# Redistributing table tiles over steps, and the order of VectorE and ScalarE work in the second pass, in a PEER layer

## What is computed

```python
q = (xb @ w_q).reshape(TOKEN_BLOCK, PEER_HEADS, 2, PEER_HALF)      # 8 heads
s1, s2 = scores of q[:, :, 0] and q[:, :, 1] with 128 keys each
v1, i1 = top_k(s1, 16); v2, i2 = top_k(s2, 16)
top_s, pos = top_k(v1[..., :, None] + v2[..., None, :], 16)
idx = i1 * 128 + i2 at pos                                          # one of 16384 experts
gate = softmax(top_s)
act = gelu(einsum('td,thkd->thk', xb, expert_u[idx]))
out = einsum('thk,thkd->td', gate * act, expert_v[idx])
x = layer_norm(alpha * x + out)
```

## Time and profile before

| | us |
|---|---|
| median of 3 runs (3006.0 to 3010.39) | 3006.27 |
| the profiled execution | 3014.1 |
| its span on the core | 3012.3 |

### The profile page before, as it was taken

How to read it: one execution, slowest core, us unless ns; L and a number is a source line. 1 busy time by engine, 2 the same in 40 slices (tenths; PEclk the granted TensorE clock), 3 DMA queues, 4 the chain that set the end, 5 groups by cost and what they waited for, 6 DMA issues and landing times. The chain is left out here.

```text
span 3012.3 us, 53462 instructions
## 1 busy us (share of the span) xinstructions
PE 2616.7 (87%) x20618; PEld 1518.2 (50%) x20618; DVE 2327.7 (77%) x4875; ACT 1223.7 (41%) x3048; POOL 971.8 (32%) x888
## 2 busy tenths in 40 slices
PE   9899978787887767768888869999998997999997
PEld 7677433232332333323333326666676775766774
DVE  7965577999879899976767867767788884877776
ACT  3254143233345555533333423333244332544454
POOL 0000144444445555544343522223232222211221
PEclk9999999889997777779998989999999999999998
DMA  4113699999999999999999989999999999999995
GB/s 165 63 56 140 240 403 419 413 404 417 412 419 405 420 411 420 419 420 421 421 418 406 419 336 383 397 394 401 400 416 375 397 412 411 386 392 369 410 393 210
DMA packets 175382, 1100.76 MB, mean 365 GB/s; under 512 B 17829, under 2 KB 34341, under 8 KB 52778
## 3 DMA queue, kind: packets, MB, share of 16 engines
q0 software_dynamic: 110592, 805.36, 65.3%
q1 hardware_dynamic: 64554, 292.16, 24.5%
HBM read 1061.79 MB, written 35.65 MB: 364 GB/s over the span
## 5 line engine op out<-in xcount | busy, mean ns | idle before, releaser
L975 POOL DMA_INDIRECT arena_high<-uv_dram,idx_now x768 | 929.3, 1210 | 1665.9 <-PE ps L1258 1525.2
L2430 DVE SCALAR_TENSOR_TENSOR arena_high<-arena_low,arena_high 128x1024 f32<-128x1024 f32 x768 | 922.4, 1223 | 267.4 <-DMA arena_high<-uv_dram,idx_now 261.5
L1258 PE MATMUL ps<-arena_high 32*32 32x512 f32 x12288 | 493.5, 671 | 282.5 <-ACT arena_high L1815 278.1
L1496 PE MATMUL ps<-arena_low 128*128 128x256 f32 x2048 | 463.7, 382 | 0.0
L1496 PEld LDWEIGHTS ps<-arena_low 128*128 128x128 f32 x2048 | 384.0, 190 | 109.4 <-issue 46.0
L1806 ACT ACTIVATE gcol<-hcol 128x2 f32<-128x2 f32 x384 | 77.6, 202 | 824.4 <-DVE arena_high L2430 820.0
L1258 PEld LDWEIGHTS ps<-arena_high 32*32 32x32 f32 x12288 | 94.8, 107 | 481.6 <-ACT arena_high L1815 384.6
L1219 PE MATMUL ps<-arena_low 128*128 128x512 f32 (+1 forms) x512 | 242.0, 616 | 14.3 <-DMA arena_low<-slabs_dram 14.3
L332 PE MATMUL ps<-wv_hi_bytes,w_hi_bytes 128*128 128x512 f32 x512 | 207.6, 406 | 19.4 <-DVE v_lo_bytes L2554 13.1
L1815 ACT ACTIVATE arena_high<-arena_high,wcol 128x32 f32<-128x32 f32 x768 | 204.9, 314 | 12.5
L334 PE MATMUL ps<-wv_hi_bytes,w_lo_bytes 128*128 128x512 f32 x512 | 202.3, 395 | 0.0
(11 more groups left out here) (264 smaller groups left out, 4002.4 us busy)
## 6 DMA issues: line engine op xcount, KB each, us to landing
arena_low<-ut_dram SPq DMA_DIRECT2D x64, 1024.0 KB
arena_high<-vt_dram SPq DMA_DIRECT2D x32, 1024.0 KB, 12.7
arena_low<-vt_dram SPq DMA_DIRECT2D x32, 1024.0 KB
arena_low<-spread_dram SPq DMA_DIRECT2D x32, 512.0 KB
acts_dram<-arena_low SPq DMA_DIRECT2D x14, 1024.0 KB
arena_low<-acts_dram SPq DMA_DIRECT2D x28, 512.0 KB
arena_low<-slabs_dram SPq DMA_DIRECT2D x11, 1152.0 KB
arena_high<-uv_dram,idx_now POOLq DMA_INDIRECT x768
```

The lines of the kernel that those rows point to most:

```text
L975: pool.indirect_dma_start(out=ring[:, s % RING, :], out_offset=None, in_=uv_d, in_offset=bass.IndirectOffsetOnAxis(ap=idx_now[:, s:s + 1], ...
L1258: last = nc.tensor.matmul(ps[out:out + QUAD, y_bank(t // PH) + turn, :], diag[rows, s % DIAGS, :], ring[rows, s % RING, cs], start=fresh, ...
L1496: last = nc.tensor.matmul(ps[:, 5 + n % 4 // 2, o:o + 2 * P], u_slot[n % USLOTS][:, k, :], x1T[:, BLK - DENSE:BLK, k, :], start=(k == 0), ...
L2430: last = nc.vector.scalar_tensor_tensor(out=ring[:, s % RING, 0:D], in0=x1[c][:, j, :], scalar=1.0, in1=ring[:, s % RING, 0:D], op0=ALU.mu ...
```

## The change

The steps are shared out anew. `TAIL` goes from 3 to 7 and `V_STEPS` from 31 to 29, which leaves `U_STEPS` = 92. The first table's tiles are no longer spread evenly: `u_share` gives a step 133, 193 or 95 parts (some 1.35, 1.96 or 0.96 tiles): 133 up to s = 55, 193 for s = 56 to 64 and 83 to 91, and 95 for s = 65 to 82. In the latter stand now all 64 groups, 18 steps instead of 24, with `hot` in 4 places, VectorE one step ahead of the other engines, and the group's work before the table tile on TensorE and ScalarE. One slab load and the first four `load_g` come earlier in SyncE's program. From s = 91 to s = 120 VectorE and ScalarE do `dense` at the beginning of a step, before the row products.

```diff
-TAIL = 3
-V_STEPS = 31
+TAIL = 7
+V_STEPS = 29
...
-G_STEP0 = PICK0 + DENSE * PH * PICK_PARTS - U0
-G_STEPS = 24
+G_STEP0 = PICK0 + DENSE * PH * PICK_PARTS - U0 + 1
+G_STEPS = 18
+HOTS = 4
 KEPT = 2
+G_BACK = G_STEP0 + G_STEPS + 4
...
+def u_share(s):
+
+    G = U0 + s
+    if G < PICK0 + 7 * STEPS:
+        return 133
+    return 95 if G_STEP0 <= s < G_STEP0 + G_STEPS else 193
+
 def u_first(s):
-    return NT * s // U_STEPS
+    return NT * sum(u_share(i) for i in range(s)) // sum(u_share(i) for i in range(U_STEPS))
...
+def second_pass(G):
+    return U_STEPS - 1 <= G - U0 < U_STEPS + V_STEPS
...
             for n in range(NT):
+                if n == USLOTS - 2:
+                    for half in range(2):
+                        load_slab_late(LATE_SLAB + 2, half)
                 if n % 2 == 0:
                     load_u(n // 2)
...
+                if n == u_first(G_BACK) + USLOTS:
+                    for c in range(2):
+                        for part in range(2):
+                            load_g(c, part)
...
-            for c in range(2):
-                for part in range(2):
-                    load_g(c, part)
...
             def dense(s):
 
-                if s == G_STEP0:
+                if s == G_STEP0 - 1:
                     for j in range(DENSE):
                         turn_picks(j)
-                if 0 <= s < U_STEPS:
-                    for n in range(u_first(s), u_first(s + 1)):
-                        u_tile(n)
                 o = s - G_STEP0
                 if 0 <= o < G_STEPS:
                     for i in range(g_first(o), g_first(o + 1)):
                         g_group(i)
+                if 0 <= s < U_STEPS:
+                    for n in range(u_first(s), u_first(s + 1)):
+                        u_tile(n)
...
+                    if second_pass(t * STEPS + g):
+                        dense(t * STEPS + g)
                     expert_weights(t, g, steps)
...
-                    dense(t * STEPS + g)
+                    if not second_pass(t * STEPS + g):
+                        dense(t * STEPS + g)
...
-                if i >= 2:
-                    wait_again(dve, g_psum, i - 1)
+                if i >= HOTS:
+                    wait_again(dve, g_psum, i - HOTS + 1)
...
-                o = s - G_STEP0
+                o = s - G_STEP0 + 1
...
+                    if second_pass(t * STEPS + g):
+                        dense(t * STEPS + g)
                     dots(t, g)
```

More of the change, by code:

```diff
@@ L418, in build @@
                  [(0, NKEY // 2, at(48, NKEY // 2, GT)), (NKEY // 2, NKEY, at(64, NKEY // 2, GT))]]
-        hot = at(16, 2, 4, 2 * P)
+        hot = [at(kib, 4, 2 * P) for kib in (16, 20, 28, 32)]
         d_onehot = at(25, TOPK, 2 * TOPK)
@@ L891, in _ @@
             for n in range(NT):
+                if n == USLOTS - 2:
+                    for half in range(2):
+                        load_slab_late(LATE_SLAB + 2, half)
                 if n % 2 == 0:
                     load_u(n // 2)
-                for i in range(LATE_SLAB + 2, len(SLABS)):
-                    s0 = (i - LATE_SLAB - 3) * STEPS
-                    if n == (USLOTS - 1 if s0 < 0 else u_first(s0 + 2) + USLOTS):
+                for i in range(LATE_SLAB + 3, len(SLABS)):
+                    s0 = (i - LATE_SLAB - 3 + 32) * STEPS - U0
+                    if n == u_first(s0 + 2) + USLOTS:
                         load_slab_late(i, 0)
-                    if n == (USLOTS - 1 if s0 < 0 else u_first(s0 + 7) + USLOTS):
+                    if n == u_first(s0 + 7) + USLOTS:
                         load_slab_late(i, 1)
@@ L1508, in g_group @@
                 for q in range(4):
-                    last = nc.tensor.matmul(ps[:, (4, 7)[i % 2], q * P:(q + 1) * P], hot[:, i % 2, q, 0:P],
-                                            hot[:, i % 2, q, P:2 * P], start=True, stop=True, skip_group_check=True)
+                    last = nc.tensor.matmul(ps[:, (4, 7)[i % 2], q * P:(q + 1) * P], hot[i % HOTS][:, q, 0:P],
+                                            hot[i % HOTS][:, q, P:2 * P], start=True, stop=True, skip_group_check=True)
                 last.then_inc(g_psum.sem, 1)
@@ L2002, in dense @@
                                              ACT.Copy).then_inc(picks_ready.sem, 1)
+                o = s - G_STEP0
+                if 0 <= o < G_STEPS:
+                    for i in range(g_first(o), g_first(o + 1)):
+                        g_group(i)
                 if 0 <= s < U_STEPS:
@@ L2006, in dense @@
                             dense_act(n - 1)
-                o = s - G_STEP0
-                if 0 <= o < G_STEPS:
-                    for i in range(g_first(o), g_first(o + 1)):
-                        g_group(i)
                 v = s - U_STEPS
@@ L2520, in hot_group @@
                     wait_again(dve, picks_ready, DENSE)
-                if i >= 2:
-                    wait_again(dve, g_psum, i - 1)
+                if i >= HOTS:
+                    wait_again(dve, g_psum, i - HOTS + 1)
                 j = i // (P // 4)
                 t0 = 4 * i - j * P
-                nc.vector.tensor_tensor(hot[:, i % 2, :, 0:P], iota128[:, :].unsqueeze(1).to_broadcast([P, 4, P]),
+                nc.vector.tensor_tensor(hot[i % HOTS][:, :, 0:P], iota128[:, :].unsqueeze(1).to_broadcast([P, 4, P]),
                                         picksT[:, j, 1, t0:t0 + 4].unsqueeze(2).to_broadcast([P, 4, P]), ALU.is_equal)
@@ L2528, in hot_group @@
                     t = t0 + q
-                    last = nc.vector.tensor_scalar(hot[:, i % 2, q, P:2 * P], iota128[:, :], picksT[:, j, 0, t:t + 1],
+                    last = nc.vector.tensor_scalar(hot[i % HOTS][:, q, P:2 * P], iota128[:, :], picksT[:, j, 0, t:t + 1],
                                                    picksT[:, j, 2, t:t + 1], ALU.is_equal, ALU.mult)
```

## The result

| | before | after |
|---|---|---|
| median, us | 3008.33 (4 runs, 3006.0 to 3013.42) | 3106.06 (4 runs, 3103.88 to 3112.1) |
| the profiled execution | 3014.1 | 3103.88 |
| its span on the core | 3012.3 | 3102.1 |

The account below looks back on a forecast made before the run. Two things were taken as full at once, TensorE (busy 87%) and the transfer engines. Terms -16 + 14 + 35 + 45 + 14 = +92 gave 3106 for the execution, 3098 as median, stated as 3095, range 3030 to 3130.

Parts of the forecast that it names:

- s = 0: Step s = 0: TensorE's 14.34 us wait for a slab and the slow start behind it go; -16 us.
- s = 1 to 63: Steps after s = 0: new shares put four more tiles here, with TensorE the bound; +14 us.
- Stores: Weights stage from s = 64: TensorE stands while ScalarE's copies wait for stores to land, 16 us each; 48 us.
- the pace: Weights stage: VectorE needs 9.8 us a step where TensorE has 8.3, in some 11 steps; 16 us.
- the clock: Weights stage: slow TensorE clock after five long waits, 2 us each; 10 us.
- The entry: Between the tables: `load_g` landed when needed, second table's first load late; some 8 of 25 us lost before remain.
- The second pass: Second table's pass, 29 steps: row products behind the rounding make TensorE wait; 464.5 us long, +45, between +21 and +73.
- The floor of 1.79: Second pass: TensorE stands 1.79 us for diagonals in each of 27 steps; with smaller waits at least 52 us.
- the 76: Second pass: waits taken as floor 52 plus about half of what late loads add up to ceiling 104; 76 us.
- The tail: Last steps, 7 for 3: VectorE's row products, sums and norms, then ScalarE and TensorE; +14 us, between +10 and +20.
- Rival (d): Weights stage and second pass: ScalarE's and VectorE's lead absorbs the waits; sum -45, 2961 us; chance 0.13.
- (b): Second pass: loads stay late, 104 us of waits, 3123; with clock cost of 1 per wait (+27, 3122), chance 0.16.

Follow-up runs that it names:

- the run with both undone: Changed kernel with row products first again in the second pass and stores of weights issued at once (+ 2 instead of + USLOTS): 3011.0 us, ratio 1.0011.
- the two last kernels: Kernel before with early slab, four places, 22 group steps, stores at once, weights' loads split two and two; first two ahead of last tile pair: 2985.97 us; behind: 2987.77.

## Why the prediction was right, and where its sizes were off

By single changes, in medians: 3008 - 18 (slab) + 11 (tail) + 46.5 (order) + 50.3 (stores) = 3098; the 8 left to 3106 (12 by the run with both undone) go with the shares and the 18 steps, which were not run alone. The forecast mechanism for each large term held.

- **s = 0** (-16): measured -18.8, and -18 alone. The half of the slab that was to cost 1.3 cost nothing visible.
- **s = 1 to 63** (+14): +11.6, with TensorE busy throughout. The four tiles more cost 13.8; the kernel before had waits of 1.14 and 1.03 in s = 62 and 63, which are gone.
- **Stores** (48): 52. Landings of 16 were assumed, 14.7 is the median. s = 79 and 81 were forecast at 15.2 and 14.1 and stood 14.3 and 16.9; store 3, forecast at nothing, cost 3.5. What was off is the pace: 16 predicted, 9.6 found, because while TensorE stands for a store VectorE works ahead; without the store waits it was 23.9. And the clock cost some 5, not 10.
- **The entry** (8): this step failed. It said that `load_g` "has landed when needed" and that of 25 lost before some 8 would remain. The step took 39.3 where 8.2 is its work: 31. It had not landed: VectorE stood 15.46 for it, and `load_g` in a row held SyncE for 18.65 with the last pair of tiles behind it. But moving it gave back little: 8 of the step in the profiled execution, 4.8 in the median, which is not told apart from nothing. Up to the landing of the last pair the transfers are full (409 GB/s), so the wait mostly moved to another load. Behind that landing they are half empty: there the new order added some 9 to 10, by the runs with the order undone and with the order alone, and this cost the sum did not have at this place.
- **The second pass** (45): 32.5. The floor of 1.79 for each step was right, 1.77. Over the bare 386 there are 65.6: 54.5 of waits and 11 of slower matmuls and small gaps (8 of these also with the old order). The step that failed is the 76, a mean between floor and a ceiling for late loads. In the longer steps (15.6 us on average for 13.5) the loads landed sooner (median 9.5 for 12.7 in the earlier trace rows), and nearly nothing of them reached TensorE: one wait of 5.29 and two of 2.9. The floor alone, 52 for the 54.5 found, would have been the forecast to take.
- **The tail** (14): 19.1. The timeline has waits of 4.13, 5.53, 2.86, 0.27, 4.10 and 4.45 for diagonals. I had summed VectorE's work; in the tail each step is a chain of norms, row products, diagonals and slow matmuls (2.02 for 1.14) in turn.
- **From execution to median**: I took 7.8 off, by which the profiled execution lay over the median; the one after lay 2.2 under its own. The sum said 3106 in the terms of the execution, which had 3103.88.

The entry, the tail and the stores were too low by 32 together, the pass and the pace with the clock too high by 24, the stages up to s = 63 by 7, TensorE's own work in the weights stage by some 3. So the total is closer than its terms, and that closeness is luck: the mechanisms of the two large terms were right, the fit of the sum, 92 for 89.8, is errors that cancel. Rival (d), that the engines' lead absorbs the waits, is refuted by the waits themselves, and the run with AHEAD 1 shows why: no lead goes around a rounding that hangs on TensorE's own tile. The clock cost of each short wait, which I held together with (b), is refuted too: the granted clock of the pass is 0.98, with a wait of 1.77 in nearly every step, and slower matmuls and gaps took 11 us with these waits for 8 without them, some 3 more and not 27.

## What to carry to other kernels

Before reordering work inside a step, find the instruction in it that waits for the engine you mean to feed, and lay out everything that then stands behind it: if that chain is longer than the engine's remaining work, the difference is paid in every step, whatever the averages say. A buffer that is refilled faster needs its store issued faster; here the store's place in the queue, written for the old pace, cost as much as the whole reordering. And a wait that vanishes under one name should be looked for under another: places for one-hots and four orders of loads changed who waited, and hardly how long.

## What was new about the hardware

- One load of 512 KB of weights in 1 KB pieces takes SyncE 0.4 us to issue, two in a row 0.93, four in a row 12.1 (in the kernel before, in the stretch of the earlier trace rows), 16.3, 18.7 and 26.0 in different kernels. Loads queued behind were held too: 10.40 for one pair, and in the two last kernels single loads of weights took 2.5 to 3.2 and pairs up to 13.4. The issue of a transfer is thus not always cheap, and what stands behind it in the list pays. That it is as slow as the transfers still under way is a likely reading, not a shown one.
- With two such loads ahead of it, a 1 MB load that otherwise lands in some 10 us (9.6 on the page after) was followed by its user only 32.8 us after its issue. GpSimd issued eight gathers in that time.
- Landing times differ with what else goes on: the second table's pairs landed in 12.7 us (median) before, 9.5 with the longer steps, 11.1 with the order undone.
